# Attention values' high and low halves added before the turn, two heads to a turned tile

## What is computed

```python
p = softmax(where(k_pos <= q_pos, (q * dh ** -0.5) @ k.T, -inf))
ya = p @ v                                  # 8 heads of 64, side by side: 512 columns
ya = rms_norm(ya, attn_out_g) * silu(az)
y = concatenate([ya, ym]) @ w_out
x = x + rms_norm(y, post_norm_g)
```

## Time and profile before

| what | value |
|---|---|
| median of 3 runs | 317.52 us (317.5 to 319.88) |
| the profiled execution's own time | 317.54 us |
| its span, first to last instruction | 315.8 us |
| PE busy | 308.7 us, 98% |
| DVE busy | 226.0 us, 72% |
| ACT busy | 165.2 us, 52% |
| POOL busy | 95.7 us, 30% |
| PE's mean granted clock | 0.997 |

### The profile page before, as it was taken

How to read it: one execution, slowest core, us unless ns; L and a number is a source line. 1 busy time by engine, 2 the same in 40 slices (tenths; PEclk the granted TensorE clock), 3 DMA queues, 4 the chain that set the end, 5 groups by cost and what they waited for, 6 DMA issues and landing times.

```text
span 315.8 us, 4994 instructions
## 1 busy us (share of the span) xinstructions
PE 308.7 (98%) x1598; PEld 255.9 (81%) x1598; DVE 226.0 (72%) x509; ACT 165.2 (52%) x337; POOL 95.7 (30%) x118
## 2 busy tenths in 40 slices
PE   8999999999999999999999999999999999999992
PEld 4788888888888888888888888778888888888882
DVE  2544999658997699968998468964576767856534
ACT  3448857287455224663157563384556876353301
POOL 4701006057340213002320025592711984000000
PEclk9999999999999999999999999999999999999998
DMA  7941543956725486645774432210120473310111
GB/s 221 326 102 33 165 138 99 169 162 161 121 67 161 126 153 199 193 128 120 184 225 149 102 95 71 77 67 27 68 67 0 131 195 148 130 69 0 69 66 67
DMA packets 29081, 38.30 MB, mean 121 GB/s; under 512 B 3624, under 2 KB 15184, under 8 KB 29056
## 3 DMA queue, kind: packets, MB, share of 16 engines
q1 hardware_dynamic: 27424, 34.51, 36.7%
q0 software_dynamic: 1472, 3.34, 7.1%
q10 hardware_dynamic: 160, 0.14, 0.1%
HBM read 33.68 MB, written 4.29 MB: 120 GB/s over the span
## 4 chain that ended last, share of the span: by engine, by line
PE 93%; issue 3%; DMA 1%; DVE 1%; DVEq 0%; ACT 0%; POOLq 0%; POOL 0%; SPq 0%; ACTq 0%
PE bank L1499 24%; PE bank L1501 24%; PE bank L1500 24%; PE bank L1551 4%; PE bank L1849 3%; PE bank L1793 3%; PE bank L1814 3%; PE bank L1646 2%; PE bank L1743 1%; DMA w_raw<-in_w_in 1%; PE bank L1532 1%; PE bank L1804 1%; PE bank L1647 1%; PE bank L1585 1%; PE bank L1586 1%
## 5 line engine op out<-in xcount | busy, mean ns | idle before, releaser
L786 ACT ACTIVATE w_hi<-w_raw 128x512 fp32r<-128x512 f32 x71 | 43.7, 626 | 63.7 <-PE bank L1501 51.0
L1499 PE MATMUL bank<-w_hi,xT_hi 128*128 128x512 f32 (+1 forms) x180 | 72.5, 403 | 0.0
L1501 PE MATMUL bank<-w_hi,xT_lo 128*128 128x512 f32 (+1 forms) x180 | 69.7, 387 | 0.0
L1500 PE MATMUL bank<-w_lo,xT_hi 128*128 128x512 f32 (+1 forms) x180 | 69.4, 385 | 0.0
L1059 DVE TENSOR_TENSOR w_lo<-w_raw,w_hi 128x512 fp32r<-128x512 f32 x64 | 45.9, 728 | 10.4 <-ACT w_hi L786 10.3
L1499 PE MATMUL bank<-xT_hi,w_hi 128*128 128x512 f32 x128 | 50.8, 397 | 0.0
L1501 PE MATMUL bank<-xT_hi,w_lo 128*128 128x512 f32 x128 | 50.1, 392 | 0.0
L1500 PE MATMUL bank<-xT_lo,w_hi 128*128 128x512 f32 x128 | 50.0, 390 | 0.0
L1501 PEld LDWEIGHTS bank<-w_hi,xT_lo 128*128 128x128 f32 x180 | 33.8, 188 | 7.2
L1499 PEld LDWEIGHTS bank<-w_hi,xT_hi 128*128 128x128 f32 x180 | 33.9, 188 | 5.8 <-issue 0.4
L1500 PEld LDWEIGHTS bank<-w_lo,xT_hi 128*128 128x128 f32 x180 | 34.0, 189 | 5.5
(11 more groups left out here) (215 smaller groups left out, 582.6 us busy)
## 6 DMA issues: line engine op xcount, KB each, us to landing
w_raw<-in_w_in SPq DMA_DIRECT2D x72, 256.0 KB, 3.1
w_raw<-in_w_out SPq DMA_DIRECT2D x16, 256.0 KB, 2.8
kq_rows<-stage SPq DMA_DIRECT2D x8, 256.0 KB
gy<-kq_rows SPq DMA_DIRECT2D x8, 256.0 KB, 3.5
gy<-in_x SPq DMA_DIRECT2D x4, 512.0 KB, 5.6
out_y<-gy SPq DMA_DIRECT2D x7, 256.0 KB, 2.1
farena<-in_x SPq DMA_DIRECT2D x4, 256.0 KB, 4.7
farena<-in_x SPq DMA_DIRECT2D x2, 512.0 KB, 6.7
```

The costliest lines, as they stand in the source:

```text
L786: a.activation(hi, raw, ACT.Copy).then_inc(w_hi_done, 1)
L1499: pe.matmul(o, hi, m_hi, start=start, stop=False)
L1500: pe.matmul(o, hi, m_lo, start=False, stop=False)
L1501: return pe.matmul(o, lo, m_hi, start=False, stop=stop)
```

## The change

High and low values of a head are added before the turn. Of `y2` (rows 0 to 63 high, 64 to 127 low, two units), ACT copies the low rows of the first unit to rows 0 to 63 of a new tile `fold`, and the high rows of the second unit to rows 64 to 127 (`fold_move`, two copies of 64x128, in odd steps behind `exp_of`). DVE adds what stands in the same rows of `y2`: high rows of the first unit, low rows of the second (`fold_sum`, two additions of 64x128, in even steps behind `mask`). `fold` then holds two heads, 64 rows each, and is turned as one tile, in odd steps. Eight heads so fill bank 3, and `ya_wide` multiplies the bank by the reciprocals in one DVE operation; `ya_half` and POOL's `ya_norm` go away for the wide tiles. Tile i = 3 does as before, but both halves in one step (`ya_last`, step 34). The `ya` events of wide tiles move by one step (square, scale, gate), the turn of tile 2 from step 33 to 34, and the parts of output tile 2 are placed differently in steps 34 and 35.

```diff
-LAG_T, LAG_PV, LAG_FOLD, LAG_YT = 2, 3, 5, 6
+LAG_T, LAG_PV, LAG_SUM, LAG_FOLD, LAG_YT = 2, 3, 5, 6, 7
...
-    (19, "ya", 0), (27, "ya", 1), (33, "ya", 2), (37, "ya", 3)])
+    (19, "ya", 0), (27, "ya", 1), (34, "ya", 2), (37, "ya", 3)])
...
-             (2, 0, [32, 32, 33, 33, 34, 34, 35, 35], 36), (2, 1, [35] * 4 + [36] * 4, 37),
+             (2, 0, [32, 32, 33, 33, 35, 35, 35, 35], 36), (2, 1, [34, 34, 34, 34] + [36] * 4, 37),
...
     _late = int(_i < NT - 1)
-    _event(_s - 3 + _late, "ya_half", _i)
-    _event(_s + 2 * _late, "ya", _i)
-    _event(_s + 3 * _late, "ya_sq", _i)
-    _event(_s + 1 + 3 * _late, "ya_ms", _i)
-    _event(_s + 1 + 4 * _late, "ya_gate", _i)
+    _event(_s + 3 * _late, "ya", _i)
+    _event(_s + 4 * _late, "ya_sq", _i)
+    _event(_s + 1 + 4 * _late, "ya_ms", _i)
+    _event(_s + 1 + 5 * _late, "ya_gate", _i)
...
+        fold = sb("fold", [P, 2, P])
...
-            def ya_norm(i):
-
-                yv = ya[:, i % 2, :].rearrange("p (h d) -> p h d", h=AH)
-                g.wait_ge(rrec_done, i + 1)
-                g.wait_ge(ya_summed, 2 * i + 2)
-                g.tensor_tensor(yv, yv, rrec[:, AH * i:AH * i + AH].unsqueeze(2).to_broadcast([P, AH, DH]),
-                                ALU.mult).then_inc(ya_done, 1)
...
+            def fold_move(u):
+
+                at = u // 2 % 2
+                a.wait_ge(y2_done, u + 2)
+                if u >= 4:
+                    a.wait_ge(yt_ps, u // 2 - 1)
+                for q in range(2):
+                    to, of = slice(q * DH, (q + 1) * DH), slice((1 - q) * DH, (2 - q) * DH)
+                    a.activation(fold[to, at, :], y2[of, q, :], ACT.Copy).then_inc(fold_moved, 1)
...
                 if s < NU:
                     exp_of(s)
+                if 0 <= s - LAG_SUM < N_WIDE and s % 2 == 1:
+                    fold_move(s - LAG_SUM)
...
             def y2_sum(u):
 
                 v.wait_ge(pv_ps, u + 2)
                 if u:
-                    v.wait_ge(yt_ps, u)
+                    v.wait_ge(fold_done, u)
...
+            def fold_sum(u):
+
+                at = u // 2 % 2
+                v.wait_ge(fold_moved, u + 2)
+                for a in range(2):
+                    half = slice(a * DH, (a + 1) * DH)
+                    v.tensor_tensor(fold[half, at, :], y2[half, a, :], fold[half, at, :], ALU.add).then_inc(fold_done, 1)
...
+            def ya_wide(i):
+
+                rec = rrec[:, AH * i:AH * i + AH]
+                v.reciprocal(rec, rsum[:, AH * i:AH * i + AH]).then_inc(rrec_done, 1)
+                v.wait_ge(yt_ps, AH // 2 * (i + 1))
                 v.wait_ge(rrec_done, i + 1)
-                v.wait_ge(ya_summed, 2 * i + 2)
+                ya_free(i)
+                v.tensor_tensor(ya[:, i % 2, :].rearrange("p (h d) -> p h d", h=AH),
+                                bank[3][:].rearrange("p (h d) -> p h d", h=AH),
+                                rec.unsqueeze(2).to_broadcast([P, AH, DH]), ALU.mult).then_inc(ya_done, 1)
...
                 if s < NU:
                     mask(s)
-                if 0 <= s - LAG_FOLD < N_WIDE and s % 2 == 1:
-                    y2_sum(s - LAG_FOLD)
+                if 0 <= s - LAG_SUM < N_WIDE and s % 2 == 1:
+                    y2_sum(s - LAG_SUM)
+                if 0 <= s - LAG_FOLD < N_WIDE and s % 2 == 0:
+                    fold_sum(s - LAG_FOLD)
...
             def turn_y2(u):
 
-                h = u % AH
-                pe.wait_ge(y2_done, u + 1)
-                if h % 4 == 0 and u:
-                    pe.wait_ge(ya_summed, u // 4)
-                pe.transpose(bank[3][:, h % 4 * P:(h % 4 + 1) * P], y2[:, u % 2, :], ident[:]).then_inc(yt_ps, 1)
+                n = u // 2
+                pe.wait_ge(fold_done, u + 2)
+                if n and u % AH == 0:
+                    pe.wait_ge(ya_done, u // AH)
+                pe.transpose(bank[3][:, n % 4 * P:(n % 4 + 1) * P], fold[:, n % 2, :], ident[:]).then_inc(yt_ps, 1)
...
                 elif h == 4:
-                    pe.wait_ge(ya_summed, 2 * (NT - 1))
+                    pe.wait_ge(ya_done, NT - 1)
...
-                if 0 <= s - LAG_YT < N_WIDE and s % 2 == 0:
+                if 0 <= s - LAG_YT < N_WIDE and s % 2 == 1:
                     turn_y2(s - LAG_YT)
-                    turn_y2(s - LAG_YT + 1)
```

More of the change, by code:

```diff
@@ L125 @@
 EVENTS = {}
-PRIORITY = ("mz", "mz_late", "z", "slot", "z_part", "part", "part_q", "ya_half", "ya", "ya_sq", "ya_ms",
+PRIORITY = ("mz", "mz_late", "z", "slot", "z_part", "part", "part_q", "ya", "ya_sq", "ya_ms",
             "ya_gate", "y_sq", "y", "y_q_sq", "y_q", "y_fin", "y_end", "cut", "turn")
@@ L472, in build @@
         y2_done = sem("y2_done")
+        fold_moved = sem("fold_moved")
+        fold_done = sem("fold_done")
         yt_ps = sem("yt_ps")
@@ L735, in _ @@
                         cut(i)
-                    elif kind == "ya" and i < NT - 2:
-                        ya_norm(i)
                     elif kind == "ya_ms":
@@ L1344, in z_gate @@
                                        op1=ALU.mult).then_inc(ym_gated, 1)
[L1346 to L1357, removed]
             def y2_sum(u):
@@ L1381, in pt_low, with ya_free, ya_last @@
                                 ALU.subtract).then_inc(pt_lo, 1)
[L1383 to L1392, removed]
-                v.wait_ge(rrec_done, i + 1)
-                v.wait_ge(ya_summed, 2 * i + 2)
-                yv = ya[:, i % 2, :].rearrange("p (h d) -> p h d", h=AH)
+            def ya_free(i):
+                if i >= 2:
+                    v.wait_ge(ssa_done, i - 1)
+                    v.wait_ge(ya_gated, i - 1)
+            def ya_wide(i):
+                rec = rrec[:, AH * i:AH * i + AH]
+                v.reciprocal(rec, rsum[:, AH * i:AH * i + AH]).then_inc(rrec_done, 1)
+                v.wait_ge(yt_ps, AH // 2 * (i + 1))
+                v.wait_ge(rrec_done, i + 1)
+                ya_free(i)
+                v.tensor_tensor(ya[:, i % 2, :].rearrange("p (h d) -> p h d", h=AH),
+                                bank[3][:].rearrange("p (h d) -> p h d", h=AH),
+                                rec.unsqueeze(2).to_broadcast([P, AH, DH]), ALU.mult).then_inc(ya_done, 1)
+            def ya_last():
+                i = NT - 1
+                yv = ya[:, i % 2, :].rearrange("p (h d) -> p h d", h=AH)
+                ya_free(i)
+                for q in range(2):
+                    v.wait_ge(pv_ps, AH * i + 4 * q + 4)
+                    v.tensor_reduce(yv[:, 4 * q:4 * q + 4, :], bank[2 + q][:].rearrange("p (h a d) -> p h d a", h=4, a=2),
+                                    mybir.AxisListType.X, ALU.add).then_inc(ya_summed, 1)
+                    if q == 0:
+                        v.wait_ge(prob_done, NU)
+                        v.reciprocal(rrec[:, AH * i:AH * i + AH], rsum[:, AH * i:AH * i + AH]).then_inc(rrec_done, 1)
+                v.wait_ge(rrec_done, i + 1)
+                v.wait_ge(ya_summed, 2)
                 v.tensor_tensor(yv, yv, rrec[:, AH * i:AH * i + AH].unsqueeze(2).to_broadcast([P, AH, DH]),
@@ L1476, in _ @@
                 for kind, what in events:
-                    if kind == "ya_half":
-                        ya_half(*what, 0)
+                    if kind == "ya" and what[0] < NT - 1:
+                        ya_wide(*what)
                     elif kind == "ya":
-                        ya_whole(*what)
+                        ya_last()
                     elif kind == "ya_ms":
```

## The result

The changed kernel is slower: 322.42 us against 317.73 us for the kernel before in the same comparison, a ratio of 1.0142 with a 95% interval of 1.0107 to 1.0177. The prediction was 317.4 us with a range of 316.1 to 318.7, so the measured time lies outside it, 5.0 us above the forecast. The profiled execution took 321.65 us, with a span of 319.9 us against 315.8.

What follows compares the result with a forecast made beforehand. PE, busy for 98% of the span, was taken as the bound. 317.54 us less 1.32 for turns saved, plus waits of 1.0 (step 17) and 0.2 (step 23), gave 317.42, predicted as 317.4, range 316.1 to 318.7.

Steps and rivals of the forecast that it cites:

- The saving: On PE in the attention stage: 12 folded tiles turned in place of 24 tiles, 0.11 us each, 1.32 us saved.
- the size of the additions and their cover: DVE, even steps behind the mask: 0.45 to 0.6 us a pair, hidden while DVE waits for ACT; free in step 16.
- ya_gate: DVE, moved to step 16 between pt_low and the mask: taken as 0.99 us, bounds 0.66 to 1.32.
- the sum for step 17: DVE from z_gate at 251.80 to y2_sum's end at 255.17; PE, ready at 254.18, waits 1.0 us (0.66 to 1.32).
- Rival C: Step 16: an addition waits for a POOL operation of 1.41 us, half counted; 318.1 us, up to 319.1; chance 0.22.
- The copies on ACT: ACT, odd steps behind the exponential: 24 copies of 64x128, 0.45 us a pair, ends 0.35 and 0.8.
- The term of steps 22 and 23: ACT's square of ya(1), 0.62 us, precedes the output bank's square, delaying y2_sum; PE waits 0.2 us (0 to 0.5).
- The last tile: Its turn on PE keeps 1.0 us of slack after its gate, 2.4 with the two moved parts; no cost.
- within 1%: Whole kernel: time within 1% (3.2 us) of the kernel before, chance 0.92.
- The 4.5 us of new waits: PE's new waits needed for the whole kernel to be slower by over 1%, chance 0.05.

Runs made afterwards that it cites:

- e2: Changed kernel with POOL's 16 output-weight subtractions cut to 1 column of each 128: 318.07 us, ratio 1.0006 to the kernel before.
- e8: Changed kernel with one-input sums over a third slot beside y2, ACT's squares swapped, ya_gate of tile 0 in step 17: 317.99 us, ratio 0.999.
- e10: e8, but with the two-input addition from unit 16 on: 318.41 us, ratio 0.9996 to the kernel before.
- e1: Changed kernel with each of the 24 fold additions replaced by a DVE sum with one SBUF input (folded values not right): 318.81 us, ratio 1.0011.
- e5: Kernel before plus 24 two-input DVE additions of 64x128 on an otherwise unused tile, nothing else of the change: 323.43 us, ratio 1.0143.
- e6: Kernel before with only the change's moved ya events, turn of tile 2 and output part order: 319.81 us, ratio 1.0045.
- e7: Changed kernel with ACT squaring the output bank before ya in a step with both: 321.99 us, ratio 1.0104 to the kernel before.

## Why the prediction was wrong

**The saving was right.** "Twelve fewer save 12 x 0.11 = 1.32 us": by step 16 seven turns fewer should give 0.77; e2, e8 and e10 show 0.73 or 0.74.

**What failed is the size of the additions and their cover.** The step said "0.45 to 0.6 us for a pair" and "fold_sum(10) itself is free there". The price was read from a subtraction with one PSUM input, and the room of 0.5 us was measured for it. In step 16 the pair took 2.39 us, so z_gate started at 253.94 in place of the predicted 251.80, and then took 1.67. The end of y2_sum, worked out as 255.17, came at 258.24 (257.56 + 0.68). Of these 3.07 us, 2.14 are z_gate's later start, 0.72 its length (1.60 from start to start where I took 0.88) and 0.21 ya_gate's (1.20 in place of 0.99). e1 and e2 show by two ways that this is the collision with POOL, e5 that the additions alone suffice.

**The rest of the sum for step 17 holds in e1.** With additions that don't collide, z_gate starts at 251.79 and PE waits 0.95 us, where 251.80 and 1.0 were predicted. In part that is luck: z_gate's length there is 0.72 from start to start and ya_gate's 1.24, where I had taken 0.88 and 0.99.

**Rival C had the mechanism and the place, at half its price.** It let one of the two additions wait for one POOL operation, and took half of that. Measured, each of the two waited for one, and z_gate behind them for another. C as written gave 318.1, its upper end 319.1, and the range was cut at 318.7, below an end that I had worked out. What misled me was one row: z_gate's 0.96 us under POOL's load, a loss of only 0.28. The row beside it, ya_gate with a loss of 0.6, was as much evidence. The operations of the earlier trace rows one by one settle it:

```profile
249.12 1.29 POOL L685 TENSOR_TENSOR w_lo<-w_raw,w_hi 128x512 fp32r<-128x512 f32 x1
...
250.36 1.75 POOL L685 TENSOR_TENSOR w_lo<-w_raw,w_hi 128x512 fp32r<-128x512 f32 x1
```

In the earlier trace rows ya_gate ends at 250.95 and z_gate at 252.66, 0.54 and 0.55 us behind the POOL operation in which each began (250.41 and 252.11), just as in the changed kernel. z_gate lost little because it began 0.41 us before the end of POOL's operation. So the loss depends on where in the other operation it begins, and the next two-input operation right behind meets a fresh one nearly whole. The average of 1.41 us that I had used for a POOL operation also hid this: those that ran without hindrance took 1.3 us, those that began inside ya_gate or z_gate 1.75 and 1.73. Of the rule from "SBUF — State Buffer", section "Who interferes with whom", in the Trainium skill, both halves held: all operations that suffered have two SBUF inputs, and those with a PSUM input kept their times. (That POOL's reading of SBUF matters, and not its writing, no run here separates.)

**ya_gate stayed inside its bounds, above the middle that I took.** It took 1.20 us from start to start, between 0.66 and 1.32, in place of 0.99. e6 prices the moved events in step 17 at 0.79 in the kernel before, though by a shorter ya_gate and an evacuation 0.42 us later, which I had put at 0.1.

**The copies on ACT** took 0.64 us a pair, where I took 0.45 and kept 0.8 as an end; the two don't overlap. No wait of PE is traced to them.

**The term of steps 22 and 23 was mis-sized.** "0.2 us of waiting (0 to 0.5)" measured 1.0 in the changed kernel (e7 removes just that), 0.8 in e2 and 0.67 in e6. The mechanism is the named one, but the squares stand 0.82 us apart, so y2_sum is later than I had worked out. Behind y2_sum the low part of the turned tile is late as well, and the scores of step 24, whose code waits for it, start 0.15 us after it ends (273.37 against 273.22); that this is the part of the loss that falls in step 24 is read from the order of events, not tried.

**The last tile was right:** from step 24 to the end the changed kernel's shift grows by 0.08 us, so its waits there are 0.19 with the last saved turn, and no wait of PE is traced to the turn of the last tile.

**A cost was missing altogether:** PE's clock. I had priced a wait of PE at its length. With a wait of 2.7 us the whole loss can be twice that, when the clock is granted at half afterwards, as in e7. How much of the changed kernel's median this makes stays open: its profiled execution (321.65 us) kept the full clock and lies below the median of 322.42, and two of its three longest (323.19 and 325.47 us) have a mean granted clock of 0.993 and 0.994, but the kernel before has 0.994 too among its shortest. The profiled execution without any fall is already 4.1 us over the kernel before, so the clock is not needed to explain that the prediction failed.

The chance of 0.92 for "within 1%" rested on the same sums. The 4.5 us of new waits, to which I gave 0.05, were passed: 5.16 us by the table, 3.35 of them in step 17, 1.0 in steps 23 and 24 and 0.6 before step 17.

## What to carry over

Before putting DVE operations with two SBUF inputs into a stretch, look at what POOL does there. If it subtracts tiles in SBUF without a break, as here, price the first at what may be left of POOL's operation, and each one right behind it at one whole POOL operation (about 1.3 us for an addition that takes 0.29 alone). Where there is a choice, give DVE one input from PSUM, or a sum over one tensor in place of an addition of two (0.42 us in all 24 places of e8, in place of 0.29 or 1.3). And when PE is the bound, an event moved by one step costs what stands behind it on each queue it enters: count the accumulator's read with its operation.

## What was not expected of the hardware

- A DVE addition of 64x128 that meets a POOL subtraction ends about 0.16 us behind POOL's operation (252.61 against 252.45), and the next one waits again: 1.08 and 1.28 us in place of 0.29. An operation of 128x512 ends 0.54 or 0.55 us behind, in the four cases above. POOL's operation that begins inside one of those takes 1.72 to 1.75 us in place of 1.3.
- After the same wait of 2.7 us PE's granted clock stayed at 1.00 in one trace (the changed kernel) and fell to 0.50 for 6 us in another (e7).
- An fp32 product with 64 columns ran as two matmuls with a weight load of 193 ns each, against one with 141 ns for a turn of 128 columns.
- ACT copies of 64x128 between partitions took 309 ns on average, and a pair 0.64 us from first start to last end: they don't overlap.
